# Rows of the normalised operand 1280 bytes apart in a two-block transformer kernel

## The reference

```python
h = h + 0.5 * _swiglu(_rmsnorm(h, ffn1_norm), ffn1_w_in, ffn1_w_out)        # x 2
x = x + 0.5 * g1 * swiglu(modulate(rms_norm(x, ln), sh, sc), wg, wu, wd)    # x 4
def swiglu(h, wg, wu, wd):
    return (jax.nn.silu(h @ wg) * (h @ wu)) @ wd
```

## Time and profile before

| | |
|---|---|
| timed runs, median (lowest to highest) | 1509.7 us (1507.81 to 1510.53), 3 runs |
| the profiled execution, its time | 1507.29 us |
| its span, first to last instruction | 1505.5 us |
| PE busy (9258 matmuls) | 1473.1 us, 98% |
| weight loads (PEld) busy | 1314.9 us, 87% |
| VectorE busy | 1177.2 us, 78% |
| ScalarE busy | 820.0 us, 54% |
| GpSimd busy | 49.6 us, 3% |
| moved from and to HBM | 341.69 MB, 227 GB/s over the span |
| mean granted TensorE clock | 0.998 |

### The profile page before, as it was taken

One profiled execution on the slowest core, in us unless ns is written; L12 is line 12 of the kernel. 1 busy time (PEld: TensorE's weight loads), 2 busy tenths in 40 slices (PEclk: granted clock), 3 DMA queues, 4 the chain that ended last, 5 costly groups with the idle time before them and its releaser, 6 DMA issues.

```text
span 1505.5 us, 22326 instructions
## 1 busy us (share of the span) xinstructions
PE 1473.1 (98%) x9258; PEld 1314.9 (87%) x9258; DVE 1177.2 (78%) x1394; ACT 820.0 (54%) x998; POOL 49.6 (3%) x40
## 2 busy tenths in 40 slices
PE   7999999899999999999999899999999999999998
PEld 6888889898888998888888888889888889988887
DVE  6988889689889778889767798898866566786654
ACT  6655354575553575554577665555655445565442
POOL 1000015200000000000000000000000000000000
PEclk9999999999999999999999999999999999999999
DMA  8988955279889559889534398897655555465551
GB/s 287 310 295 287 339 194 167 84 250 313 297 284 330 178 191 303 296 289 311 168 113 142 128 304 294 288 325 253 191 188 182 184 166 169 141 221 180 186 184 68
DMA packets 275972, 341.69 MB, mean 227 GB/s; under 512 B 6931, under 2 KB 256939, under 8 KB 275872
## 3 DMA queue, kind: packets, MB, share of 16 engines
q1 hardware_dynamic: 273904, 334.74, 67.3%
q0 software_dynamic: 1968, 5.54, 1.1%
HBM read 339.18 MB, written 2.63 MB: 227 GB/s over the span
## 4 chain that ended last, share of the span: by engine, by line
PE 86%; DVE 7%; ACT 4%; issue 1%; DMA 1%; DVEq 0%; SPq 0%; ACTq 0%
PE banks L1691 43%; PE banks L1692 22%; PE banks L1623 5%; PE banks L1624 5%; PE banks L1625 5%; DVE w_lo L993 1%; ACT w_hi L536 1%; DVE xn L1064 1%; DVE ada_acc L1111 1%; ACT xs L566 1%; DVE x_res L1137 1%; PE banks L1763 1%; ACT xn L555 1%; DVE xs L1012 1%; DMA ada<-in_ada_w 0%
## 5 line engine op out<-in xcount | busy, mean ns | idle before, releaser
L1691 PE MATMUL banks<-xs,w_hi 128*128 128x512 f32 x1952 | 682.7, 393 | 3.2 <-DVE w_lo L993 3.0
L993 DVE TENSOR_TENSOR w_lo<-raw,w_hi 128x2048 fp32r<-128x2048 f32 (+1 forms) x241 | 537.9, 2237 | 161.5 <-ACT w_hi L536 161.3
L536 ACT ACTIVATE w_hi<-raw 128x2048 fp32r<-128x2048 f32 (+1 forms) x249 | 464.8, 1870 | 214.9 <-PE banks L1692 169.7
L1692 PE MATMUL banks<-xs,w_lo 128*128 128x256 f32 x1952 | 547.6, 281 | 0.0
L1691 PEld LDWEIGHTS banks<-xs,w_hi 128*128 128x128 f32 x1952 | 366.4, 188 | 88.4 <-DVE w_lo L993 4.3
L1691 PE MATMUL banks<-g_pair,w_hi 128*128 128x512 f32 x1056 | 366.9, 391 | 0.0
L1692 PEld LDWEIGHTS banks<-xs,w_lo 128*128 128x128 f32 x1952 | 366.8, 188 | 0.0
L1692 PE MATMUL banks<-g_pair,w_lo 128*128 128x256 f32 x1056 | 295.7, 280 | 0.0
L1691 PEld LDWEIGHTS banks<-g_pair,w_hi 128*128 128x128 f32 x1056 | 197.5, 187 | 43.2
L1692 PEld LDWEIGHTS banks<-g_pair,w_lo 128*128 128x128 f32 x1056 | 199.6, 189 | 0.0
L1111 DVE SCALAR_TENSOR_TENSOR ada_acc<-ada,c_act,ada_acc 128x1152 f32<-128x1152 f32 x124 | 175.2, 1413 | 12.3 <-DMA ada<-in_ada_w 9.7
(11 more groups left out here) (302 smaller groups left out, 1694.9 us busy)
## 6 DMA issues: line engine op xcount, KB each, us to landing
ada<-in_ada_w SPq DMA_DIRECT2D x128, 576.0 KB, 6.9
raw<-in_ffn_wg SPq DMA_DIRECT2D x44, 1024.0 KB, 5.5
raw<-in_ffn_wu SPq DMA_DIRECT2D x44, 1024.0 KB, 5.5
raw<-in_ffn_w_in SPq DMA_DIRECT2D x43, 1024.0 KB, 7.1
raw<-in_ffn_wd SPq DMA_DIRECT2D x32, 1024.0 KB, 5.2
raw<-in_ffn_w_out SPq DMA_DIRECT2D x16, 1024.0 KB, 6.4
raw<-in_ffn_wd SPq DMA_DIRECT2D x16, 768.0 KB, 4.9
raw<-in_attn_w_qkv SPq DMA_DIRECT2D x12, 1024.0 KB, 5.3
```

The lines of the kernel that those rows point to most:

```text
L536: act.activation(w_hi[:, s, 0:width(c)], raw[:, s, 0:width(c)], ACT.Copy).then_inc(hi_ready, 1)
L993: dve.tensor_tensor(w_lo[:, s, 0:width(c)], raw[:, s, 0:width(c)], w_hi[:, s, 0:width(c)].bitcast(F32), ALU.subtract).then_inc(lo_ready, 1)
L1691: pe.matmul(o, wh[:, k, m], pair, start=first, stop=False, skip_group_check=True)
L1692: return pe.matmul(o[:, 0:T], wl[:, k, m], pair[:, 0, :], start=False, stop=last, skip_group_check=True)
```

## The change

`XS_ROW` becomes 320 floats: rows of `xs` are 1280 bytes apart. `xs` grows by 3072 bytes a partition. To make room, `ada` has 3584 floats instead of 4096, `consts` keeps three matrices, and the three masks get a place of their own at the end of `arena`, loaded by a second DMA. `b_mix`, which lay at the end of `ada`, moves into `arena`. The waits for the constants count 32 instead of 16. The filling matmuls read the three remaining matrices, 384 columns instead of 512.

```diff
@@ -126,7 +126,7 @@
 NCOLS = _at
 
 
-XS_ROW = T + 16
+XS_ROW = T + 64
 X_PARTS = 4
 SKEW = 384
 
@@ -158,14 +158,14 @@
         arena = sb("arena", [P, ARENA])
         xn = sb("xn", [P, KT, T])
         ub = sb("ub", [P, KT, T])
-        ada_flat = sb("ada", [P, 4 * D])
+        ada_flat = sb("ada", [P, 14 * T])
         ada_acc = sb("ada_acc", [P, ADA_W])
         silu_g = sb("silu_g", [P, 2 * T])
         gu = sb("gu", [P, 2 * T])
         rstd = sb("rstd", [P, 2 * T])
         cols = sb("cols_sb", [P, NCOLS])
-        consts = sb("consts_sb", [P, 6, P])
-        tri, low_mask, up_mask, ident, causal, pair_ones = (consts[:, i, :] for i in range(6))
+        consts = sb("consts_sb", [P, 3, P])
+        ident, causal, pair_ones = (consts[:, i, :] for i in range(3))
         ones_d = sb("ones_d", [P, P])
         ones_c = sb("ones_c", [P, P])
         ones_v = sb("ones_v", [P, P])
@@ -203,6 +203,8 @@
         glr = carve(T, 32)
         wup = carve(T, 32)
         w_glr = carve(KT * 16).rearrange("p (k n) -> p k n", k=KT)
+        masks = carve(3 * P).rearrange("p (i n) -> p i n", i=3)
+        tri, low_mask, up_mask = (masks[:, i, :] for i in range(3))
 
         top[0] = 0
         conv_y = carve(CT * T).rearrange("p (c t) -> p c t", c=CT)
@@ -238,7 +240,8 @@
 
         ln_rows = ada_flat[:, 0:2 * D].rearrange("p (a n) -> p a n", a=2)
         w_mix = ada_flat[:, 2 * D:2 * D + KT * P].rearrange("p (g t) -> p g t", g=KT)
-        b_mix = ada_flat[0:2, 2 * D + KT * P:2 * D + 2 * KT * P]
+        top[0] = KEPT
+        b_mix = carve(KT * P, 2)
         top[0] = 0
         v_g = carve(2 * D).rearrange("p (a n) -> p a n", a=2)
         b_hi, b_pair = (w[0:2, 0:4, :].rearrange("p a n -> p (a n)") for w in (cs_hi, cs_lo))
@@ -484,7 +487,8 @@
             pool.dma_start(table[0:NB, :], a["rel_bias_2"]).then_inc(ev("table_in"), 16)
             pool.dma_start(one_hot, a["one_hot"]).then_inc(ev("table_in"), 16)
             pool.dma_start(lam_in[:, 0:4], a["lam"]).then_inc(ev("lam_in"), 16)
-            pool.dma_start(consts[:, :, :], a["consts"]).then_inc(consts_in, 16)
+            pool.dma_start(consts[:, :, :], a["consts"][:, 3:6, :]).then_inc(consts_in, 16)
+            pool.dma_start(masks, a["consts"][:, 0:3, :]).then_inc(consts_in, 16)
 
             pool.wait_ge(ev("rows_copied"), 1)
             pool.dma_start(bias_rows, rows).then_inc(ev("rows_out"), 16)
@@ -1386,7 +1390,7 @@
                 folded(1)
                 conv(6)
 
-                dve.wait_ge(consts_in, 16)
+                dve.wait_ge(consts_in, 32)
                 chosen(0)
                 dve.wait_ge(ev("kv_done"), 1)
                 dve.wait_ge(ev("decay"), 1)
@@ -1730,7 +1734,7 @@
 
             def norm(n, after=False, within=False):
                 if n and not after:
-                    pe.wait_ge(consts_in, 16)
+                    pe.wait_ge(consts_in, 32)
                 if JOINT[n]:
                     return
                 d = deferred(n)
@@ -1768,7 +1772,7 @@
                 elif n and not after and d is None:
 
                     for _ in range(FILL):
-                        pe.matmul(bank[MISC][:, :], ones_d[:, :], consts[:, 0:4, :], start=True, stop=True,
+                        pe.matmul(bank[MISC][:, 0:3 * P], ones_d[:, :], consts[:, :, :], start=True, stop=True,
                                   skip_group_check=True)
 
             def ffn(n):
```

## The result

| | before | after |
|---|---|---|
| timed runs, median (lowest to highest) | 1509.07 us (1507.81 to 1510.53), 6 runs | 1519.58 us (1510.92 to 1525.25), 6 runs |
| ratio after / before, 95% interval | | 1.0063 [1.0033, 1.0093] |
| the profiled execution, its time and span | 1507.29, 1505.5 us | 1520.27, 1518.5 us |
| mean granted TensorE clock | 0.998 | 0.996 |

What follows compares the result with a forecast made beforehand. The prediction took PE, busy in 98% of the span, as the bound. Pairs -4.9, triples +2.5 and small forms +0.2 gave -2.2 us, moving the median from 1509.7 to 1507.5 us, range 1503.5 to 1512.0.

Steps and rivals of the forecast that it cites:

- The bound: Whole kernel: PE, busy 98% of the span, stays the bound, with VectorE and DMA still covering it.
- the transfer rival: Feed-forward stages: DMA engines at 0.97 hold them, so only the triples' loss is left, 1512.4 us; chance 0.05.
- Pairs on `xs`: Feed-forward matmuls on `xs`: 1952 pairs go from 349.2 to the 346.7 ns of `g_pair`, -4.9 us.
- a slow position: Pairs on `xs`: slowest position of the old spacing pattern, 0.36 us; as price of every pair, +21 us.
- `g_pair` at zero: Pairs on `g_pair`, whose addresses the change leaves alone: expected to stay as they are, at 346.7 ns.
- Triples, +2.5 on the path: Three-matmul helper `mm3` on `xs`: 360 ns as on `cs`, +2.8 us in all, +2.5 on the path.
- Only the pairs move: Rival: triples on `xs` stay where they are and only the pairs gain 4.9 us, 1504.8 us; chance 0.14.
- Filling, constants, masks, `b_mix`: Shorter filling matmuls, second constants DMA and moved tensors: cost or give nothing; filling shrinks 0.4 to 0.5 us into a wait.
- Small forms: Smaller matmul shapes, such as those of 258 columns: +0.2 us together, between -0.3 and +0.6.
- The clock: Sign of a wrong prediction: a clock drop appearing behind the shorter filling matmuls.
- Spacing doesn't hang on rows: Rival: matmul spacing comes from something else, such as weight order or semaphores, so nothing moves, 1509.7 us; chance 0.09.
- Odd rows are another kind: Rival: every second `xs` row, 256 past a multiple of 512, is slow; pairs average 350.4 ns, 1514.7 us; chance 0.09.

Runs made afterwards that it cites:

- both64: Changed kernel with `xs` rows and the weight tiles both 64 bytes further on; 1517.5 us, ratio 1.0057 to the kernel before.
- old_stride: Changed kernel with only the row spacing undone (`XS_ROW = T + 16`), the rest of the change kept; 1508.25 us, ratio 0.9998 to the kernel before.
- after_again: Changed kernel run once more with no edit; 1518.22 us, ratio 1.0074 to the kernel before.
- lead192: Changed kernel with every row of `xs` 192 bytes further on; 1518.72 us, ratio 1.007 to the kernel before.
- kick: Changed kernel plus a 64-column matmul into an unread bank before each up-projection chunk from the fifth on; 1528.22 us, ratio 1.013 to the kernel before.
- mixed64: Changed kernel with 1088-byte `xs` rows in feed-forwards, 1280-byte rows 64 bytes further on elsewhere; 1507.42 us, ratio 0.9993 to the kernel before.
- best1: Changed kernel with 1088-byte `xs` rows in feed-forwards; other stages' `xs`, `cs` and `p` at distance 192; 1505.17 us, ratio 0.9975 to the kernel before.
- row7: Changed kernel with one `xs` row of eight 64 bytes further on; 1518.78 us, ratio 1.0069 to the kernel before.

## Why the prediction was wrong

Forecast 1507.5 us, range 1503.5 to 1512.0; the median is 1519.6, outside it and on the other side of before. For the profiled span the sum said -2.2 us, and it grew by 13.0: 8.4 of the difference are the pairs on `xs`, 4.7 those on `g_pair`, 2.3 the clock.

- **The bound** was read rightly. PE is the whole path, VectorE and DMA cover it (idle in front of the 1952 pairs 3.2, then 3.6 us), and the transfer rival did not occur.
- **Pairs on `xs`, -4.9 us: the step that failed.** It took the 346.7 ns of `g_pair` for the price of a constant distance. That is one of two prices. The quick level did come, at the 346.7 forecast, and 353 came in the other stages; the mean 351.0 made it +1952 x 1.8 = +3.5. The other price was not to be read from before: its `g_pair` is quick in all six stages, and the forecast took one stretch of 120 pairs from them. What it lacked was a reason to think that a constant distance has a single price. The text held the bounds of a slow position, 0.36 us, but counted them as a position in a pattern of four rows, not as a state that a constant distance could have.
- **`g_pair` at zero: the second failed step.** "As they are" followed from its unchanged addresses. But the level at which `g_pair` starts depends on the pairs in front: quick each time behind the old rows, and whatever `xs` ended on behind rows at distance 0. So it cost 4.7 us, more than `xs` itself. The next stage pays for what the edited operand starts.
- **Triples, +2.5 on the path:** right in mechanism and size. 360.0 ns against 355.0, 283 ns each, and 360.0 with `xs` as the stationary operand as well. *Only the pairs move* is refuted by them, and by `both64`.
- **Filling, constants, masks, `b_mix`:** right, by `old_stride` at 0.9998. **Small forms:** the 96 matmuls of 258 columns in the first of their lines are busy 25.8 us as before. Rows of after:

```profile
202.70 1.45 PE L1775 MATMUL banks<-consts_sb,ones_d 128*128 128x384 f32 x4
204.93 0.35 PE L1648 MATMUL banks<-xs,w_hi 128*128 128x256 f32 x1 [0.78 <-ACT xs L632]
...
3.90 0.54 POOL L491 DMA_DIRECT2D arena<-in_consts  x1
...
arena<-in_consts POOLq DMA_DIRECT2D x1, 192.0 KB, 6.8
```

  The filling (two calls, recorded as four matmuls) is 1.45 us instead of 1.88 and the wait behind it 0.78 instead of 0.36; the second DMA is issued at 3.90 and lands 6.8 us later, at 10.7.
- **The clock** stood among the signs of an error, and it did come: 2.3 us of longer stretches at 1.2 GHz. They are at 284 and 847 us, not behind the shortened filling at 203, and `after_again` had one only; what the change has to do with them is open.
- ***Spacing doesn't hang on rows*** is refuted: `old_stride` takes the loss back whole, and `lead192` moves triples from 360.0 to 340.0 with nothing but an address. By the Trainium skill's N / 2.4 GHz plus 2.5 ns ("TensorE: Matmul & The Clock Gate", section "Wait — 56ns, not 53.3ns?") an estimate for three matmuls of 256 columns is 327.5 ns. The runs don't agree: the least that any stretch here showed is 340.0.
- ***Odd rows are another kind*** named the right sign and a mean of 350.4 ns, close to the measured 351.0, but that is luck, for the mechanism is another: neighbouring rows don't alternate, whole stages do, and `g_pair`, none of whose rows lies off a multiple of 512, slows as well. It was given 0.09. Its turning point is 347.8 ns a pair by the prediction's own terms (349.2 - 2.7 / 1952), not 348.0, which changes nothing.

**Open.** What picks the level at a break; in `kick` it goes by a period of three chunks. Why rows at 64, and the old rows, leave the following `g_pair` at its quick level (24 times of 24 in before, `old_stride`, `mixed64` and `best1`), where 128 and 192 leave it at the slow one and one odd row in eight (`row7`) does so in five stages of six. Whether the up-projections themselves can be held at the quick level: `kick` could not. That it is two orders in which weight loads and row reads meet is an idea that no row here shows.

## What to carry to other kernels

Where PE is the bound, read the start-to-start spacing of every long stage, in more than one profile, before calling a spacing the price of an operand: a mean can be two levels, and the level of a stage can depend on the stage in front. The distance between the moving operand and the weights, modulo 256 bytes, is worth trying like a tile size, for each form of matmul by itself. Changing the form with it, three matmuls of 256 columns at a distance of 192 instead of 512 + 256 at any, brought 1.1% to a kernel that was 98% PE.

## What the runs showed of the hardware

All at the 2.4 GHz level, fp32r, a weight tile for every matmul, no idle time; ns for each pair (512 + 256 columns) or triple (3 x 256):

| distance, modulo 256 bytes | triple | pair |
|---|---|---|
| 0 | 360.0 | 346.7 or 353.3 |
| 64 | 353.3 or 340.0 | 348.9 or 353.3 |
| 128 | 356.0 | 351.1 |
| 192 | 340.0 or 353.3 | 353.3 |
| changing row by row (1088-byte rows) | 355.0 | 349.2 |

- Same columns, same engine load, up to 20 ns in 360 by address alone.
- Where two levels stand in a cell, either holds without a change as long as the matmuls follow each other at the same distance, for more than 100 pairs. The same program falls into different ones in different executions: shown for pairs at distance 0, the only case traced twice.
- Where pairs at distance 0 follow others without a break, the distance of those in front picks their level: 346.7 behind 64 (six of six), 353.3 behind 128 and 192 (six of six each), the same as in front behind 0.
- What can change it is small: 64 columns of another matmul, a few transposes, a wait of 1.3 us.
